# Twenty-two more 128x512 transposes by VectorE's 32x32 squares and transfers on the chip instead of TensorE, in a kernel of three transformer blocks

## What is computed

```python
# first block, layer 1
q, k, v, gate, qi, ki, wi = jnp.split(h @ w_in, ATTN_SPLITS, axis=-1)
q = rope_partial(q.reshape(B, L, 16, 128), positions, 32)   # k alike
logits = einsum('bqhd,bqkhd->bhqk', q, k_sel)                # q and k with features on the rows
x = x + gate * ((o * silu(gate)) @ w_out)                    # then rms_norm, and the second block
# second block
proj = rmsnorm(x, norm_mix_pre) @ w_in
qk = silu(causal_depthwise_conv(concat([mq, mk]), conv_w, conv_b))   # over positions, each feature alone
aq_h = apply_rope(to_heads(aq, 8), positions)                # ak alike; moba_attention(aq, ak, av)
merged = sigmoid(g_m) * (h_m @ w_branch_m) + sigmoid(g_a) * (h_a @ w_branch_a)
x = x + rmsnorm(merged @ w_out, norm_mix_post)
u = square(relu(rmsnorm(x, norm_ffn_pre) @ w_up)); y = u @ w_down
```

## Time and profile before

| | us |
|---|---|
| runs | 2376.49, 2376.66, 2375.19 |
| median | 2376.49 |
| the profiled execution | 2376.75 |
| its span, first to last instruction | 2374.9 |
| TensorE busy | 2326.1 |
| VectorE busy | 1528.7 |
| ScalarE busy | 1117.7 |
| GpSimd busy | 140.4 |

### The profile page before, as it was taken

The page is one execution under the profiler, slowest core; times in us unless marked ns, Lnnn a source line. Parts: engine busy times, 40 slices in busy tenths (PEclk is TensorE's granted clock), DMA queues, the critical chain, the costliest instruction groups (busy, mean ns, idle before and its releaser), DMA issues.

```text
span 2374.9 us, 30018 instructions
## 1 busy us (share of the span) xinstructions
PE 2326.1 (98%) x10902; PEld 1888.6 (80%) x10902; DVE 1528.7 (64%) x1863; ACT 1117.7 (47%) x1347; POOL 140.4 (6%) x277
## 2 busy tenths in 40 slices
PE   5999999999999999999999999999999999999998
PEld 1877777888788878888888888888888888888886
DVE  2988887666697556875765444665665665565566
ACT  1444445444444455545444444454554444454454
POOL 0000000000000000000000000000131121121120
PEclk8999999999999999999999999999999999999999
DMA  9999996555597546656454766556566666666663
GB/s 392 386 377 378 376 398 250 181 178 176 191 382 268 169 157 196 224 160 188 133 185 151 238 193 190 179 198 196 177 213 208 201 211 204 203 209 195 209 208 110
DMA packets 253414, 536.59 MB, mean 226 GB/s; under 512 B 25068, under 2 KB 25332, under 8 KB 249336
## 3 DMA queue, kind: packets, MB, share of 16 engines
q1 hardware_dynamic: 241520, 510.40, 63.6%
q0 software_dynamic: 10128, 22.07, 2.7%
q10 hardware_dynamic: 1656, 2.65, 0.3%
HBM read 520.35 MB, written 6.30 MB: 222 GB/s over the span
## 4 chain that ended last, share of the span: by engine, by line
PE 93%; DVE 3%; DMA 2%; ACT 1%; issue 1%; ACTq 0%; DVEq 0%; SPq 0%
PE ps L1924 29%; PE ps L1926 29%; PE ps L1925 29%; PE ps L1994 2%; DMA ifb<-in_f_bias 1%; PE ps L2024 1%; PE ps L2203 0%; DMA T<-in_mod_w 0%; DVE w_lo L1057 0%; PE ps L2244 0%; PE ps L2103 0%; PE ps L2180 0%; ACT tmp L807 0%; PE ps L2246 0%; PE ps L2245 0%
## 5 line engine op out<-in xcount | busy, mean ns | idle before, releaser
L1057 DVE TENSOR_TENSOR w_lo<-raw,w_hi 128x1024 fp32r<-128x1024 f32 x784 | 944.9, 1217 | 527.9 <-ACT w_hi L524 513.5
L524 ACT CAST w_hi<-raw 128x1024 fp32r<-128x1024 f32 x784 | 815.7, 1046 | 875.0 <-PE ps L1926 827.5
L1924 PE MATMUL ps<-w_hi,xa_hi 128*128 128x512 f32 x2176 | 855.4, 393 | 5.3 <-DVE w_lo L1057 3.1
L1926 PE MATMUL ps<-w_hi,xa_lo 128*128 128x512 f32 x2176 | 847.5, 389 | 0.0
L1925 PE MATMUL ps<-w_lo,xa_hi 128*128 128x512 f32 x2176 | 846.9, 389 | 0.0
L1924 PEld LDWEIGHTS ps<-w_hi,xa_hi 128*128 128x128 f32 x2176 | 408.6, 188 | 99.5 <-issue 11.0
L1926 PEld LDWEIGHTS ps<-w_hi,xa_lo 128*128 128x128 f32 x2176 | 408.5, 188 | 85.9
L1925 PEld LDWEIGHTS ps<-w_lo,xa_hi 128*128 128x128 f32 x2176 | 408.7, 188 | 82.6
L1924 PE MATMUL ps<-w_hi,xb_hi 128*128 128x512 f32 x928 | 364.6, 393 | 2.0 <-issue 1.3
L1926 PE MATMUL ps<-w_hi,xb_lo 128*128 128x512 f32 x928 | 361.4, 389 | 0.0
L1925 PE MATMUL ps<-w_lo,xb_hi 128*128 128x512 f32 x928 | 361.2, 389 | 0.0
(11 more groups left out here) (266 smaller groups left out, 1046.9 us busy)
## 6 DMA issues: line engine op xcount, KB each, us to landing
raw<-in_w_in SPq DMA_DIRECT2D x176, 512.0 KB, 3.9
T<-in_mod_w SPq DMA_DIRECT2D x160, 512.0 KB, 7.7
raw<-in_attn_w_in SPq DMA_DIRECT2D x144, 512.0 KB, 4.5
raw<-in_w_up SPq DMA_DIRECT2D x128, 512.0 KB, 4.2
raw<-in_w_down SPq DMA_DIRECT2D x128, 512.0 KB, 4.5
raw<-in_pool_w_in SPq DMA_DIRECT2D x64, 512.0 KB, 8.0
T<-in_mod_w SPq DMA_DIRECT2D x16, 1024.0 KB, 8.9
raw<-in_pool_w_out SPq DMA_DIRECT2D x32, 512.0 KB, 8.9
```

What stands on the lines that cost most here:

```text
L524: nc.scalar.copy(w_hi[:, o % SPL, :, 0:cols], raw[:, o % RAW, :, 0:cols]).then_inc(hi_ready, 1)
L1057: tt(w_lo[:, o % SPL, :, part], raw[:, o % RAW, :, part], w_hi[:, o % SPL, :, part].bitcast(F32), ALU.subtract).then_inc(lo_ready, 1)
L1924: mm(dst, x_hi, h, start=first and k == 0, stop=False)
L1926: ins = mm(dst, x_lo, h, start=False, stop=last and k == KPC - 1)
```

## The change

The 22 jobs of `qk` (8), `attn_out` (the first 3), `m_qk` (4), `a_qk` (4) and `branch` (the first 3) become turns by squares. TensorE no longer has them. VectorE's hook that left the job's result now makes the square transpose, after waiting until the turn before has landed. POOL gets the loops of 16 transfers between its other transfers (two stores and loads of the residual, three rows that are spread). ScalarE waits for the landing and unfolds `gathered` to the job's former target (`unfold`), or scales it (`norm2_split`), or casts it (`split_gathered`). The convolution reads the unfolded copy `conv_u` in SBUF instead of PSUM, two columns after chunk 9 and two after chunk 10. The last jobs of `attn_out` and `branch` stay on TensorE. A table `TURNS` counts turns.

```diff
+            def cross(src, dst, landed):
+
+                for a in range(4):
+                    for f in range(4):
+                        pool.dma_start(dst[32 * f:32 * f + 32, a, :, :], src[32 * a:32 * a + 32, f, :, :]).then_inc(landed, 16)
+
+            def turns(name, jobs, src, dst):
+
+                for b in range(jobs):
+                    pool.wait_ge(turn_ready, TURNS[name] + b + 1)
+                    cross(src, dst, turn_landed)
...
+            def unfold(name, b, src, dst):
+
+                act.wait_ge(*turned(name, b))
+                nc.scalar.copy(dst.rearrange("p f (t a i) -> p f t a i", t=NT, a=4),
+                               src.rearrange("p a (t f) i -> p f t a i", t=NT)).then_inc(unfolded, 1)
...
+            with act.Fori(1, n) as b:
+                blk(b + B0, {8: lambda: index_relu(b), 10: lambda: qk_unfold(b - 1)})
                 to_qk(b, b + B0, b + A0)
-            phase("gate", lambda b, B, A: evac(T2[:, :, bass.ds(b * NBLK, NBLK)], A, B * CPB + CPB, ACT.Silu))
+            phase("gate", lambda b, B, A: evac(T2[:, :, bass.ds(b * NBLK, NBLK)], A, B * CPB + CPB, ACT.Silu),
+                  first={10: lambda: qk_unfold(7)})
...
+            for b in range(1, n):
+                blk(B0 + b, {6: lambda: attn_squares(b - 1), 10: lambda: norm2_split(b - 1)})
+                attn_out(b, B0 + b, A0 + b)
...
-                    {}, {5: lambda: conv_silu(0)}, {5: lambda: conv_silu(1)})):
+                    {8: lambda: conv_unfold(0)}, {5: lambda: conv_silu(0), 8: lambda: conv_unfold(1)},
+                    {5: lambda: conv_silu(1), 8: lambda: conv_unfold(2)})):
...
+            phase("a_qk", to_stage("a_qk", scale=r_mix), aqk_unfold, 10, first={8: mlstm_split(0, 6), 9: mlstm_split(1, 4)},
+                  ahead=AHEAD + 2)
...
+            def turn(name, b, dst):
+
+                if TURNS[name] or not (isinstance(b, int) and b == 0):
+                    dve.wait_ge(turn_landed, b * 256 + TURNS[name] * 256)
+                turn_blocks(dst, turn_ready)
...
             def qk_out(b):
-                leave(b + JOBS["qk"], qk_t[:, bass.ds(b * 4, 4), :])
+                turn("qk", b, blocks)
...
+            with step.loop(1, n, 2) as b:
+                blk(b + B0, {2: lambda: norm_turn(b - 1), 10: lambda: norm_low(b - 1)})
+                residual(b, b + A0)
...
+                return {2: lambda: conv_turn(b), 9: lambda: pair(0), 10: lambda: pair(2)}
...
             for b in range(1, n):
-                blk(b + B0, {7 + f: (lambda f=f: conv(b - 1, f)) for f in range(4)})
+                blk(b + B0, conv_hooks(b - 1))
...
-            with pe.Fori(1, n) as b:
-                blk(b + B0, b + A0, XB, True, {3: lambda: qk_job(b - 1), 5: lambda: index_scores(b)})
+                blk(b + B0, b + A0, XB, True, {5: lambda: index_scores(b)})
```

More of the change, by code:

```diff
@@ L143, with _turns @@
 _staged()
+TURNS = {}
+def _turns():
+    n = 0
+    for name, jobs in (("qk", 8), ("norm2", 3), ("m_qk", 4), ("a_qk", 4), ("branch", 3)):
+        TURNS[name] = n
+        n += jobs
+    return n
+N_TURNS = _turns()
 SQ = {"norm1": 2, "norm2": 10, "mlstm": 26, "mix_out": 34, "norm3": 42, "ffn": 46}
@@ L486, in _ @@
             clear(5)
+            turns("qk", 8, blocks, gathered)
             pool.wait_ge(pv_ready, DSA_HEADS)
@@ L503, in _ @@
             pool.dma_start(T3[:], tokens(resid[1])).then_inc(res_landed, 16)
+            turns("branch", 3, blocks, gathered)
             pool.wait_ge(res_done, 2)
@@ L507, in _ @@
                 pool.wait_ge(blocks_ready, n + 1)
[L508 to L511, removed]
+                cross(blocks, gathered, blocks_landed)
         @block.scalar
@@ L770, in to_stage, with stage_free @@
                 return each
+            def stage_free(name, b):
+                if name in TURNS and not (isinstance(b, int) and b == 0):
+                    act.wait_ge(turn_ready, b + TURNS[name])
+                else:
+                    act.wait_ge(tp_ready, b + JOBS[name])
             phase("idx_q", to_stage("idx_q", "norm1"),
@@ L1553, in _, with norm_turn, norm_low @@
             attention(0, 0, DSA_HEADS, "attn", pick[:], T2, 0, True, PHASES["attn_out"][0])
-            norm_out, norm_low = outs("norm2", XB, MIXP)
-            phase("attn_out", add_residual(2, T0), norm_out, norm_low, per=2, first={6: lambda: low_job(SPLITS["attn"] + 3, XA, 3, 4)},
-                  ahead=AHEAD + 2)
+            def norm_turn(b):
+                dve.wait_ge(staged, b + (STAGED["norm2"] + 1))
+                turn("norm2", b, blocks)
+            def norm_low(b):
+                low_part(b + SPLITS["norm2"], XB, b, tmp[:])
+            B0, A0, n = PHASES["attn_out"]
+            residual = add_residual(2, T0)
+            blk(B0, {6: lambda: low_job(SPLITS["attn"] + 3, XA, 3, 4)}, at=AHEAD + 2)
+            residual(0, A0)
+            with step.loop(1, n, 2) as b:
+                blk(b + B0, {2: lambda: norm_turn(b - 1), 10: lambda: norm_low(b - 1)})
+                residual(b, b + A0)
             def output_rstd():
@@ L1755, in _ @@
             B0, A0, n = PHASES["branch"]
-            out, low = outs("branch", XB)
             def branch(b, first=False):
@@ L1760, in branch @@
                 cols = bass.ds(b * NBLK, NBLK)
+                if not first:
+                    dve.wait_ge(staged, b + STAGED["branch"])
+                    turn("branch", b - 1, blocks)
                 for o in range(AHEAD, CPB + AHEAD):
                     lo(B, o)
-                    if o == 5 and not first:
-                        out(b - 1)
+                    if o == 10 and not first:
+                        low_gathered(b + (SPLITS["branch"] - 1), XB, b - 1)
                     if o == 6:
-                        if not first:
-                            low(b - 1)
                         dve.wait_ge(acc_free, A + 1)
@@ L2359, in branch @@
                         chunk(b + B0, 4 * half + j, XA, 8 * half + KPC * j, A, j == 0, j == 3)
-                    if half == 0 and not first:
-                        branch_job(b - 1)
-            branch(0, first=True)
+            branch(0)
             with pe.Fori(1, n) as b:
                 branch(b)
-            phase("mix_out", XB, first={3: lambda: branch_job(3)}, ready=SPLITS["branch"])
+            phase("mix_out", XB, first={3: lambda: job(JOBS["branch"], stage, staged, STAGED["branch"] + 4, bank=4)}, ready=SPLITS["branch"])
             X0 = SPLITS["ffn"]
```

185 lines of the change are left out of this document (107 added, 78 removed).

## The result

The changed kernel takes 2427.7 us in the median of its runs (2425.6 to 2430.8), the kernel before 2375.9 beside it: 1.0216 times as long, 95% interval 1.0203 to 1.0229. The forecast was 2420, in a range of 2382 to 2455. Its span is 2424.4, 49.5 longer than before.

The account below looks back on a forecast made before the run. TensorE, busy 98% of the span, was taken as the bound. Waits of 19 + 4 + 22 + 17 = 62 us less 19 for the removed jobs gave net +43, so 2376.75 + 43 = 2420 us, range 2382 to 2455.

Parts of the forecast that it names:

- the jobs' 0.87 us: TensorE time each removed job of eight transposes costs; 22 jobs were to free 19 us.
- The loop of the convolution: Convolution, one turn's cycle from transpose to next transpose: L + 13.6 = 28.6 us against a block of 21.8.
- L: Each turn's time from the square transpose's end to its data in place: taken as 15.0 us, ends 12.5 and 17.0.
- First heads: First attention's heads: loop L + 9.85 = 24.85 us against 22.87, excess 2.0 seven times, 14 us of waits.
- Second heads: Second attention's heads, 4 turns: loop L + 12.4 = 27.4 us against 21.8, 17 us of waits.
- The gate: Gate phase, where the first heads' eighth turn falls: no margin, 5 us more of waits.
- long rival: L long and the stall spreading, gate's DMA slice at 9 tenths, clock may fall: 2461 us and up, chance 0.10.
- The norm: Post-attention norm, 3 turns: loop L + 8.8 = 23.8 us, excess 2.0, 4 us of waits in all.
- The convolution: Convolution, 4 turns: 6.8 us excess per loop, three full loops 20, waits of 22 us in sum.
- Branches: Branches, 3 turns: loop L + 6.1 = 21.1 us, within the block, 0 waits.
- TensorE's busy time: Sign in the profile after: TensorE busy about 19 us less and idle about 60 more.
- Fast landing: Rival: transfers land fast, L at least 9.8 us, and the jobs' time is gained: 2365 us, chance 0.14.

Follow-up runs that it names:

- e_one: Changed kernel with one 512 KB transfer per turn in place of sixteen, squares not crossed between partition groups: 2364.8 us, 0.9949 of the kernel before.
- e_one_late: e_one with the ten square transposes of norm, convolution and branches moved behind the low part of chunk 3: 2363.2 us.
- e_best: Changed kernel with heads' copies later, norm's transposes behind chunk 3, transfers of norm, convolution and branches split between POOL and SyncE: 2364.6 us, 0.9951 of before.
- e_small: Changed kernel with the turns' transfers cut to an eighth of their bytes, same number of issues: 2410.8 us.

## Why the prediction was right, and where it was not

**The bound and the mechanism** held: TensorE was full, the jobs' 0.87 us came out as 0.9 per turn wherever nothing waits (-6.3 for seven), and in the changed kernel the loops set the pace. The loop of the convolution was put at L + 13.6; the three distances between its copies are 28.67, 30.13 and 28.52 with L of 14.92, 16.38 and 14.76, which is L + 13.75. First heads L + 9.85: measured L + 9.6. Second heads L + 12.4: measured 12.0 to 12.2. These terms were built from rows of the kernel before and from round prices of a copy, a cast and a column, such as 1.0 and 2.0.

**L** was taken as 15.0 for all turns; the mean of the 22 is 15.0, from 11.6 to 18.8, with 17 pauses where three of four turns were forecast. But it is not equal over the stages. In the first heads it is 13.9, so the term of 14 us of waits was twice too big (0.2 + 6.3 = 6.5). With an L of 14 it would have been 7.

**The gate** was put at 5 us of waits and is 12.6. The slack was read too high (10.0, in e_one the copy is reached after 7.1). A table load of 1.28 on ScalarE, which stands between the copy and the evacuation (679.58), had no term. And its L is 18.8 instead of 15: the pause there is 6.18, within 0.02 of the longest, and from the last issue to the last landing it takes 5.0, at a DMA share of 0.87. The 9 tenths of that slice stood in the forecast's long rival, but not in its sum. Heads and gate together came out at +11.9 for +12.0 forecast, by two errors of 8 us that cancel. Over the six stages the errors are 7.7, 7.6, 4.5, 3.2, 3.0 and 1.5, 27 us together, of which 6 are left in the sum: that 2420 came so near is in good part luck.

**The norm** was put at 4 us of waits and is 8.5. The loop was forecast as L + 8.8 and is L + 9.9 (24.81 and 26.21 between the splits, L of 14.94 and 16.35). The sum went from ScalarE's split to the evacuation to VectorE's 3.9, and left out the low part of the split (1.2), which VectorE does ahead of its work on the evacuated block. And it had no term for the square transpose ahead of the cast that is due, which e_one_late priced.

**The convolution** was put at 22, with the jobs +18.5, measured +21.7: loops 0.15 longer, and L of 15.4 in the mean. **Second heads** +13.5, measured +10.5, with L of 14.4 in the mean. **Branches**: the loop, L + 6.1, is L + 6.6, so with L of 16.5 and 18.3 two turns wait 1.5 and 4.7, which costs 1.5 of the 2.6.

**TensorE's busy time** was expected 19 less and its idle time 60 more. It is 4.7 more and 45 more. The lower clock takes some 24 us of busy time, an estimate (4.7 + 19) to which e_best, with the same instructions on TensorE and a granted clock of 0.996, answers with 22.7 (2330.8 - 2308.1). In the convolution these lie inside the loops, whose distances fit L + 13.75 with no clock in them. That it costs nothing elsewhere is only argued from this; no run holds the clock up while the waits stay.

**The rivals.** Fast landing was put at 2365 with an L of 9.8, which counts the last issue's 0.5 twice, since the rows time a landing from the start of its issue: 9.3. L is 11.5 or more in each turn that waits, so it is refuted. That e_one (2364.8) and e_best (2364.6) take the time that it gave is chance: its sum had 7 us of waits for L, and theirs have other terms. The transfers do slow themselves by about 1 us (e_small), not the weights: from 440 to 1660 us of the span ScalarE waits 2.9 us for raw weights in the changed kernel, and 36.2 before.

## What to carry to other kernels

Price a transposition that goes through many small transfers by its latency from the last input to the first use, issues and pauses included, and compare it with the slack of each place: the same turn of 15 us is free behind a whole block of 21.8 and costs 1 (first heads) to 12.6 us (gate) where an evacuation stands behind its wait. Before a faster path for the data is looked for, move the wait behind the work that others need. An instruction put ahead of one that is due can cost its own length even if all else is hidden (1.2 us for a transpose of 1.25, in two blocks of the norm).

## What the runs showed of the hardware

- POOL's issues of transfers stop for 2.7 to 6.2 us after every 21 with a ring of 1024 and after every 42 with 2048; bytes have little to do with it (67.7 us in 17 pauses with an eighth of them, 79.7 in 17 with all). Part of a pause comes back in the landing: the last transfer of a turn without one lands 4.8 to 5.2 us after its issue in the mean, with one 3.2 to 3.3.
- One issue of a 32 KB transfer between partitions takes 0.50 us on POOL and 0.65 us on SyncE; one transfer of 512 KB in place of 16 lands in 5.1 us in the median (3.1 to 8.2), while POOL's 16 of 32 KB need 11.1 at the least.
- TensorE's idle times of 2.11 and 3.44 us that stand above were followed by matmuls at 1.2 GHz, those of 1.11 and 2.86 were not. All stretches at 1.2 GHz in the changed kernel made 23 to 24 us of busy time, without a cost that could be seen beside the waits themselves.
